# Modulation vectors of a two-block transformer: the weight tiles taken in four stages instead of one, part of each tile multiplied on TensorE

## The chip, the cores and the metric

The kernel runs on one core of a Trainium2 chip. The metric is the device time of one execution in microseconds (us); lower is better. Everything is computed in 32-bit floats. The core has five engines that run their own instruction lists and meet only at semaphores: TensorE (PE; loads of its weights are listed apart as PEld), VectorE (DVE), ScalarE (ACT), GpSimd (POOL) and SyncE (SP). SP and ACT issue the transfers of this kernel.

## The reference, cut to what matters

Two transformer blocks of two layers each work on x (512 tokens by 1024). Only the first block is modulated: six vectors for each layer come from one condition vector.

```python
cond = jax.nn.silu(c)                          # (1, 1024)
for layer in range(2):
    mod = cond @ w_ada[layer] + b_ada[layer]   # w_ada: (2, 1024, 6144)
    sh1, sc1, g1, sh2, sc2, g2 = jnp.split(mod[:, None, :], 6, axis=-1)
    h = rms_norm(x, norm_mix[layer]) * (1.0 + sc1) + sh1
    y = gated_deltanet_mixer(h, ...) if layer == 0 else dilated_attention_mixer(h, ...)
    x = x + g1 * y
    h = rms_norm(x, norm_ffn[layer]) * (1.0 + sc2) + sh2
    x = x + g2 * swiglu(h, w_ffn_in[layer], w_ffn_out[layer])
```

w_ada is 48 MB, the largest single input. It is a matrix times one vector: each of its numbers is used once.

## The kernel before

The program is a chain of **stages** (`Core.stage`). In each stage every engine has one list, written out by hand; no engine starts the next stage before all have ended this one. Within a stage the order on an engine is the order of the code, and it waits only where the code says `wait_ge`. x is kept turned, channels on partitions, as 8 tiles of 128x512.

**w_ada in tiles.** A tile is 512 columns of w_ada by all 1024 rows: 128 partitions by 8 row blocks k by 512 columns, 2 MB. There are 12 tiles for each layer. `set_up` takes all 24, one after the other, before anything else is computed. ACT loads them into six buffers (`tiles`, L362). DVE multiplies row block k by `cond[:, k]` and adds up over k, even and odd k in two separate sums (`scaled`, L401 and L404, eight instructions for a tile). TensorE adds over the 128 partitions by eight matmuls with one moving column of ones (L348). Also in `set_up`: x is loaded by one transfer and turned (L323, copied by L384), small vectors are loaded in rows by 28 or so transfers on SP and turned (L331, L387), the squares of x give the first root of the norm (L301, L338, L371).

**Decay rows** (`gdn_rows`) is the second stage: the norm of layer 0 (`Norm`: a diagonal on DVE L461, a spread by TensorE L448, eight products on DVE L455, eight shifts on ACT L443), a projection to 16 columns (L885, eight for the first half `part`, then eight for the second), then a chain between ACT and DVE over the decay rows (L899 to L940), a turn on TensorE (L891) and a copy (L942). `gdn_heads` follows, and its weights are requested at its start (L974). The rest of layer 0 follows and takes until 1162 us.

**Bias stage** (`window_biases`), the first of layer 1's mixer: four matmuls make bias rows (L1546), which go out to memory and come back shifted (L1535, L1539, into `slots[0]`); in the meantime the norm of layer 1 runs; then eight matmuls flip them (L1556), DVE copies each (L1571) and adds a mask (L1575).

**Dilated attention** (`window_attention`) goes over 12 pairs of heads m, each with four blocks of 128 queries (iterations r). For each m, SP loads three weight parts (keys, queries, values) into `slots[m % 2]` (L1633). In iteration r TensorE computes the scores of r (L1698), parts of the projections of pair m+1 and m+2 (L1650, L1659, L1666) with their sums of squares (L1677) and the spread of inverse roots (L1684), the attention of r-2 (L1712) and the turn of the probabilities of r-1 (L1724). DVE does `maxima(r)` (L1855, L1859), ACT the exponents (L1796), DVE `weigh(r)` (L1865, L1868).

## Time and profile before

| | us |
|---|---|
| three timed runs | 4657.93, 4659.88, 4664.34 |
| their median | 4659.88 |
| the profiled execution | 4659.29 |
| its span, first to last instruction | 4657.5 |
| set-up stage, to 156.48 | 156.5 |
| decay rows, 156.48 to 184.06 | 27.6 |
| TensorE busy | 4303.1 (92%) |
| DVE busy | 1943.2 (42%) |
| mean granted TensorE clock | 0.932 |

[...] A 32-bit matmul is two records in the trace, so "x16" in a timeline row is eight matmuls. A timeline row merges neighbours of one kind: start, duration of the merged piece, engine, line, operation, operands, shape, count of records, and in brackets the idle time before it and what ended it. "SPq" and "ACTq" are the issuing of transfers.

### The profile page before, as it was taken

Reading aid. Unit: us, or ns where it says so; the run is one execution under the profiler, and the core shown is the slowest. Engines: PE = TensorE matmul, PEld = TensorE weight load, DVE = VectorE, ACT = ScalarE, POOL = GpSimd, SP = SyncE. Lnnn points to the kernel's source line nnn. Section 1 sums busy time; section 2 is a strip of 40 time slices with the busy share of each in tenths; the row PEclk is TensorE's granted clock in tenths of the full one; section 3 lists DMA queues with packets and bytes.
Section 4 is the critical chain, followed back from the end, with each engine's and each line's share of the span. In section 5 each row is a group of like instructions: output and inputs, shape, how many; then the busy total and the mean of one; then the engine's idle time right before and its main releaser. Section 6 shows DMA issues by size and latency. Waiting matters only on the chain. (4 is left out here: it accounts for less than half of the span.)

```text
span 4657.5 us, 51781 instructions
## 1 busy us (share of the span) xinstructions
PE 4303.1 (92%) x18256; PEld 2930.7 (63%) x18256; DVE 1943.2 (42%) x3480; ACT 897.4 (19%) x1784; POOL 1022.3 (22%) x738
## 2 busy tenths in 40 slices
PE   6799799999899789988889999999899799999998
PEld 6444696888466378874554444888645544447887
DVE  7465543332233443322347012675223570127752
ACT  0233221100233211002340101221013401002210
POOL 0000322443100034420005000444200051004443
PEclk6799899999899799998989999999899899998998
DMA  9421002322222023244112221232351132222332
GB/s 374 135 57 36 5 14 77 90 80 75 74 55 55 10 81 88 84 97 90 35 39 72 72 72 54 81 90 84 72 105 30 35 81 72 63 63 72 90 86 68
DMA packets 621097, 351.02 MB, mean 75 GB/s; under 512 B 67890, under 2 KB 591091, under 8 KB 620964
## 3 DMA queue, kind: packets, MB, share of 16 engines
q1 hardware_dynamic: 593188, 297.12, 24.3%
q10 hardware_dynamic: 27776, 52.18, 3.0%
q8 instruction: 78, 1.28, 0.1%
q14 instruction: 55, 0.45, 0.0%
HBM read 339.77 MB, written 2.13 MB: 73 GB/s over the span
## 5 line engine op out<-in xcount | busy, mean ns | idle before, releaser
L676 PE MATMUL psum<-h_normed,weight_slot 128*128 128x256 f32 x2816 | 645.6, 383 | 16.9 <-DMA weight_slot<-in_ffn_w_up 7.9
L228 PE MATMUL psum<-h_normed,weight_slot 128*128 128x512 f32 x1408 | 610.0, 596 | 18.4 <-DMA weight_slot<-in_w_in 18.4
L676 PEld LDWEIGHTS psum<-h_normed,weight_slot 128*128 128x128 f32 x2816 | 540.5, 192 | 98.0 <-issue 23.1
L228 PEld LDWEIGHTS psum<-h_normed,weight_slot 128*128 128x128 f32 x1408 | 269.1, 191 | 357.5 <-issue 357.5
L676 PE MATMUL psum<-sums_in,weight_slot 128*128 128x256 f32 x2112 | 485.0, 379 | 5.6 <-POOL weight_slot L650 5.6
L644 POOL TENSOR_TENSOR weight_slot<-weight_slot 128x512 f32<-128x512 f32 (+1 forms) x136 | 173.2, 1273 | 1415.5 <-DMA weight_slot<-in_w_ffn_in 837.8
L676 PEld LDWEIGHTS psum<-sums_in,weight_slot 128*128 128x128 f32 x2112 | 400.9, 190 | 61.5 <-POOL weight_slot L650 7.2
L739 DVE COPY work<-psum 128x256 f32<-128x256 f32 x104 | 43.8, 421 | 618.7 <-PE psum L676 618.7
L2883 DVE SCALAR_TENSOR_TENSOR u<-raw,vectors,u 128x511 f32<-128x511 f32 (+1 forms) x176 | 214.9, 1240 | 99.7 <-ACT u L2862 86.6
L2144 PE MATMUL psum<-h_normed,weight_slot 128*128 128x512 f32 x576 | 252.5, 600 | 2.6 <-ACT o_swa L2333 2.6
L676 PE MATMUL psum<-sums_hidden,weight_slot 128*128 128x256 f32 x1056 | 243.8, 379 | 0.0
L983 PE MATMUL psum<-h_normed,weight_slot 128*128 128x512 f32 x512 | 232.6, 610 | 11.5 <-DMA weight_slot<-in_gdn_w_in 11.5
L676 PEld LDWEIGHTS psum<-sums_hidden,weight_slot 128*128 128x128 f32 x1056 | 200.5, 190 | 27.6 <-POOL weight_slot L650 0.5
L2144 PEld LDWEIGHTS psum<-h_normed,weight_slot 128*128 128x128 f32 x576 | 110.1, 192 | 141.6 <-issue 141.4
L650 POOL TENSOR_TENSOR weight_slot<-weight_slot 128x512 f32<-128x512 f32 (+1 forms) x136 | 185.8, 1366 | 10.7
L983 PEld LDWEIGHTS psum<-h_normed,weight_slot 128*128 128x128 f32 x512 | 98.3, 195 | 134.3 <-issue 134.3
L646 POOL TENSOR_TENSOR weight_slot<-weight_slot 128x512 f32<-128x512 f32 (+1 forms) x136 | 179.7, 1321 | 10.7
L648 POOL TENSOR_TENSOR weight_slot<-weight_slot 128x512 f32<-128x512 f32 (+1 forms) x136 | 179.5, 1320 | 10.7
L2729 POOL TENSOR_TENSOR x_residual<-x_residual,h_normed 128x512 f32<-128x512 f32 x16 | 19.9, 1272 | 714.9 <-DVE h_normed L2717 714.9
L676 PE MATMUL psum<-conv_ffn_hidden,weight_slot 128*128 128x256 f32 x704 | 160.1, 379 | 0.0
L676 PE MATMUL psum<-ffn_hidden,weight_slot 128*128 128x256 f32 x704 | 160.1, 379 | 0.0
L2635 DVE SCALAR_TENSOR_TENSOR o_conv<-padded,vectors,o_conv 128x512 f32<-128x512 f32 x240 | 159.2, 743 | 0.0
(395 smaller groups left out, 5883.5 us busy)
## 6 DMA issues: line engine op xcount, KB each, us to landing
tiles<-in_w_ada ACTq DMA_DIRECT2D x24, 2048.0 KB, 15.2
weight_slot<-in_w_ffn_in SPq DMA_DIRECT2D x88, 512.0 KB, 4.9
weight_slot<-in_ffn_w_up SPq DMA_DIRECT2D x88, 512.0 KB, 4.8
weight_slot<-in_w_gate SPq DMA_DIRECT2D x64, 512.0 KB, 4.7
weight_slot<-in_w_in SPq DMA_DIRECT2D x40, 512.0 KB, 4.9
weight_slot<-in_dsw_w_in SPq DMA_DIRECT2D x36, 512.0 KB, 5.4
weight_slot<-in_gdn_w_in SPq DMA_DIRECT2D x32, 512.0 KB, 6.7
weight_slot<-in_w_ffn_out SPq DMA_DIRECT2D x64, 256.0 KB, 3.5
```

Source lines behind the costliest of these rows:

```text
L228: last = c.nc.tensor.matmul(c.ps[:, 4 * s + t, :], weights(c.slots[s], t, k), moving(k), start=(k == 0), stop=(k == kt - 1))
L644: nc.gpsimd.tensor_tensor(b(self.S1), b(self.A21), b(self.A22), ALU.add).then_inc(self.folded, 1)
L646: nc.gpsimd.tensor_tensor(b(self.S2), b(self.S1), b(self.A11), ALU.subtract).then_inc(self.folded, 1)
L648: nc.gpsimd.tensor_tensor(b(self.S3), b(self.A11), b(self.A21), ALU.subtract).then_inc(self.folded, 1)
L650: nc.gpsimd.tensor_tensor(b(self.S4), b(self.A12), b(self.S2), ALU.subtract).then_inc(self.folded, 1)
L676: last = nc.tensor.matmul(c.ps[:, 4 * bank + r // 2, (r % 2) * self.HALF:(r % 2 + 1) * self.HALF], c.slots[s][:, b * 512 + k * P:b * 512 + ...
L739: nc.vector.tensor_copy(u4, p(self.P1)).then_inc(self.link, 1)
L983: last = nc.tensor.matmul(c.ps[:, t, :], c.slots[s][:, (t * KT + k) * P:(t * KT + k + 1) * P], c.h[:, k, :], start=(k == 0), stop=(k == KT ...
L2144: last = nc.tensor.matmul(c.ps[:, BANK_OF[t], :], c.slots[j % 2][:, (i * KT + k) * P:(i * KT + k + 1) * P], c.h[:, k, :], start=(k == 0), ...
L2635: nc.vector.scalar_tensor_tensor(o_conv[:, t, :], padded[:, t, ds(k, S)], c.vec[:, ds(layer * (CONVW * CT) + k * CT + (cw + t), 1)], o_con ...
L2729: nc.gpsimd.tensor_tensor(c.x[:, k, :], c.x[:, k, :], c.h[:, k, :], ALU.add).then_inc(self.pool_added, 1)
L2883: ins = nc.vector.scalar_tensor_tensor(u[:, s, t, back:], raw[:, s, t, 0:S - back], tap(i, s, t, 2 - back), u[:, s, t, back:], ALU.mult, A ...
```

## The change

- `c` is loaded by a transfer of its own, first on SP, and turned by one matmul into a bank of its own; the condition `c.cond` is now kept for the whole program. x is loaded by four transfers, one for 128 tokens each; its squares are summed on ACT.
- A tile's row blocks k = 0 to 4 are summed on DVE into one sum (`Modulation.sum_tile`: five instructions, each waiting for the one before it). For row blocks 5, 6, 7 TensorE takes the tile itself as weights and `cond[:, k]` as the one moving column (`Modulation.products`): with the sum's own matmul this makes 16 matmuls for a tile instead of 8.
- The tiles are taken in four stages: layer 0's first four (sh1, sc1) in `set_up`; its other eight in `gdn_rows`; layer 1's first four in `window_biases`; its other eight in `window_attention`, all eight row blocks on DVE there (`scale_part`, two instructions in each iteration r of the pairs m = 0 to 7), with four added matmuls for each pair m = 2 to 9 behind L1677.
- Layer 0's tiles go through a ring of seven buffers, which are the later `silu_z`, `q_decayed`, ... of the mixer. Tiles 0 to 6 are loaded by ACT, 7 to 10 by SP in `set_up`, 11 by SP in `gdn_rows`. In the bias stage ACT loads four tiles at its start. In dilated attention SP loads half tiles between the weights.
- The projection of `gdn_rows` goes over k outside and over the two halves inside, and the second half is written to PSUM partitions 64 to 71.
- The weights of the first pair of heads are requested at the end of SP's list in the bias stage (`first_window_weights`), and pair m uses `slots[(m + 1) % 2]`.

```diff
+            sp.dma_start(cond_rows[:, :], ins["c"].rearrange("a (k p) -> (a k) p", p=P)).then_inc(cond_loaded, 16)
+            sp.dma_start(c.ident[:, :], c.const("ident")).then_inc(cond_loaded, 16)
+            for t in range(TT):
+                sp.dma_start(x_rows[:, t, :], ins["x"][0, t * P:(t + 1) * P, :]).then_inc(x_loaded[t], 16)
...
+            for n in range(len(ring), ADA_FIRST + len(ring)):
+                sp.wait_ge(ada.multiplied, n - len(ring) + 1)
+                ada.load(sp, ring, n)
...
+            nc.tensor.transpose(c.ps[:, 7, 0:KT], cond_rows[:, :], c.ident[0:KT, 0:KT]).then_inc(cond_turned, 1)
...
+            for n in range(ADA_FIRST):
+                if n == 2:
+                    pe.wait_ge(vecs_loaded, 16 * len(loads))
+                    for b in range(2):
+
+                        pe.wait_ge(copied, b + 2)
+                        for t in range(4):
+                            last = nc.tensor.transpose(c.ps[:, b + 1, t * P:(t + 1) * P], vec_rows[:, 4 * b + t, :], c.ident[:, :])
+                        last.then_inc(turned, 1)
+                ada.products(pe, n, ring[n], n)
...
-            with pe.Fori(0, DEPTH * STEPS // 2) as i:
-                for s in range(2):
-
-                    pe.wait_ge(done, i * 2 + (s + 1 + ADA))
-                    for t in range(4):
-                        for part in range(2):
-                            last = nc.tensor.matmul(c.ps[:, 0, ds(i * 8 + (4 * s + t), 1)],
-                                                    scaled[:, s, part, t * P:(t + 1) * P], c.ones[:, 0:1],
-                                                    start=(part == 0), stop=(part == 1))
-                    last.then_inc(summed, 1)
...
-            with dve.Fori(0, DEPTH * STEPS // ADA) as i:
-                for s in range(ADA):
-                    n = i * ADA + s
-
-                    dve.wait_ge(loaded[s], i * 16 + 16)
-                    dve.wait_ge(summed, n + 1)
-                    for k in range(KT):
-
-                        to = scaled[:, s % 2, k % 2, :]
-                        if k < 2:
-                            ins = nc.vector.tensor_scalar(to, tiles[:, s, k, :], cond[:, k:k + 1], None, ALU.mult)
-                        else:
-                            dve.wait_ge(added, n * (KT - 1) + (k - 1))
-                            ins = nc.vector.scalar_tensor_tensor(to, tiles[:, s, k, :], cond[:, k:k + 1], to, ALU.mult, ALU.add)
-                        ins.then_inc(added if k < KT - 1 else done, 1)
...
+ADA_TILES = 12
+ADA_FIRST = 4
+ADA_REST = ADA_TILES - ADA_FIRST
+class Modulation:
+    SPLIT = 5
+    def __init__(self, c, sems, bank, scaled=None):
+        self.c, self.bank = c, bank
+        self.link, self.summed, self.multiplied = sems
+        self.scaled = c.slots[1][:, 3 * D:4 * D].rearrange("p (s n) -> p s n", s=2) if scaled is None else scaled
+    def load(self, engine, ring, n):
+        engine.dma_start(ring[n % len(ring)], columns(self.c.ins["w_ada"][n // ADA_TILES, :, :], n % ADA_TILES * 512, 512)
+                         ).then_inc(self.c.ada_loaded[n % len(ring)], 16)
+    def sum_tile(self, dve, i, tile):
+        c, nc = self.c, self.c.nc
+        to = self.scaled[:, i % 2, :]
+        if i >= 2:
+            dve.wait_ge(self.multiplied, i - 1)
+        nc.vector.tensor_scalar(to, tile[:, 0, :], c.cond[:, 0:1], None, ALU.mult).then_inc(self.link, 1)
+        for k in range(1, self.SPLIT):
+            dve.wait_ge(self.link, i * (self.SPLIT - 1) + k)
+            nc.vector.scalar_tensor_tensor(to, tile[:, k, :], c.cond[:, k:k + 1], to, ALU.mult, ALU.add
+                                           ).then_inc(self.link if k < self.SPLIT - 1 else self.summed, 1)
+    def products(self, pe, i, tile, place):
+        c, nc = self.c, self.c.nc
+        pe.wait_ge(self.summed, i + 1)
+        for t in range(4):
+            at, to = slice(t * P, (t + 1) * P), c.ps[:, self.bank, 4 * place + t:4 * place + t + 1]
+            for k in range(self.SPLIT, KT):
+                nc.tensor.matmul(to, tile[:, k, at], c.cond[:, k:k + 1], start=(k == self.SPLIT), stop=False)
+            last = nc.tensor.matmul(to, self.scaled[:, i % 2, at], c.ones[:, 0:1], start=False, stop=True)
+        last.then_inc(self.multiplied, 1)
+    def add_bias(self, dve, first, n, place):
+        c, b = self.c, self.c.column("b_ada")
+        return c.nc.vector.tensor_tensor(c.mod[:, 4 * first:4 * (first + n)], c.ps[:, self.bank, 4 * place:4 * (place + n)],
+                                         c.vec[:, b + 4 * first:b + 4 * (first + n)], ALU.add)
...
-            for part in range(2):
-                for k in range(KT):
-                    pe.wait_ge(norm.ready, k + 1)
-                    last = nc.tensor.matmul(c.ps[0:GH, part, :], w_ab[:, k, part * GH:(part + 1) * GH], c.h[:, k, :],
+            for k in range(KT):
+                pe.wait_ge(norm.ready, k + 1)
+                for part in range(2):
+                    last = nc.tensor.matmul(c.ps[64 * part:64 * part + GH, part, :], w_ab[:, k, part * GH:(part + 1) * GH], c.h[:, k, :],
                                             start=(k == 0), stop=(k == KT - 1))
-                last.then_inc(projected, 1)
+            last.then_inc(projected, 1)
+            for i in range(REST // 2):
+                ada.products(pe, i, tile_of(i), i)
 
             pe.wait_ge(rows_stacked, 4)
             for t in range(TT):
                 last = nc.tensor.transpose(c.ps[:, 2, t * P:(t + 1) * P], stacked[:, t * P:(t + 1) * P], c.ident[:, :])
             last.then_inc(turned, 1)
+            for i in range(REST // 2, REST):
+                ada.products(pe, i, tile_of(i), i)
...
+            for i in range(ADA_FIRST):
+                ada.products(pe, i, ring[i], i)
             norm.tensor(pe)
             pe.wait_ge(spread, 64)
 
-            pe.wait_ge(norm.ready, KT)
-            for h in range(WH):
+            for h in (0, 1, 2, 3, 6, 7, 5, 4):
 
                 if h < 4:
                     pe.wait_ge(copied, h + 1)
+                if h == 5:
+                    pe.wait_ge(biased, 1)
+                if h == 4:
+                    pe.wait_ge(norm.ready if norm.shift is None else norm.scaled, KT)
                 nc.tensor.matmul(c.ps[:, h, :], flip[:, :], falling[:, h, :, :].rearrange("p j n -> p (j n)"),
...
+            for i in range(ADA_FIRST):
+                act.dma_start(ring[i], columns(c.ins["w_ada"][1, :, :], i * 512, 512)).then_inc(c.ada_loaded[i], 16)
...
+            for i in range(ADA_FIRST):
+                dve.wait_ge(c.ada_loaded[i], 16 * (landed[i] + 1))
+                ada.sum_tile(dve, i, ring[i])
+            dve.wait_ge(ada.multiplied, ADA_FIRST)
+            ada.add_bias(dve, ADA_TILES, ADA_FIRST, 0).then_inc(biased, 1)
+            dve.wait_ge(biased, 1)
+            modulated_gain(c, 1, 0).then_inc(biased, 1)
+            dve.wait_ge(biased, 2)
             norm.vector(dve)
...
+            def load_half(j, half):
+                if j:
+                    sp.wait_ge(taken, 2 * (j - 1) + half + 1)
+                w = columns(c.ins["w_ada"][1, :, :], (ADA_FIRST + j) * 512, 512)
+                sp.dma_start(tile[:, half, :, :], w[:, half * (KT // 2):(half + 1) * (KT // 2), :]).then_inc(half_loaded[half], 16)
+
+            window_weights(c, sp, 1, w_loaded[1])
+            load_half(0, 0)
+            load_half(0, 1)
+            for m in range(2, NM):
+                sp.wait_ge(v_projected, m - 1)
+                if 3 <= m < ADA_REST + 2:
+                    load_half(m - 2, 0)
+                window_weights(c, sp, m, w_loaded[m % 2])
+                if 3 <= m < ADA_REST + 2:
+                    load_half(m - 2, 1)
...
+                if part == 1 and 2 <= m < ADA_REST + 2:
+                    last = sum_tile(m - 2)
                 last.then_inc(summed, 1)
+
+            def sum_tile(j):
+
+                pe.wait_ge(ada_summed, j + 1)
+                for t in range(4):
+                    last = nc.tensor.matmul(c.ps[:, SUMS, 16 + t:17 + t], scaled[:, j % 2, t * P:(t + 1) * P], c.ones[:, 0:1],
+                                            start=True, stop=True)
+                return last
...
+            def scale_part(r):
+                j, b = r // TT, r % TT
+                half = b // 2
+                to = scaled[:, j % 2, :]
+                if b % 2 == 0:
+                    dve.wait_ge(half_loaded[half], 16 * (j + 1))
+                if b == 0 and j >= 2:
+                    dve.wait_ge(summed, 2 * j + 2)
+                for k in range(2 * b, 2 * b + 2):
+                    col, row = c.cond[:, k:k + 1], tile[:, half, k % (KT // 2), :]
+                    if k == 0:
+                        nc.vector.tensor_scalar(to, row, col, None, ALU.mult).then_inc(ada_link, 1)
+                        continue
+                    dve.wait_ge(ada_link, j * KT + k)
+                    ins = nc.vector.scalar_tensor_tensor(to, row, col, to, ALU.mult, ALU.add).then_inc(ada_link, 1)
+                dve.wait_ge(ada_link, j * KT + 2 * b + 2)
+                if b % 2:
+                    dve.sem_inc(taken, 1)
+                if b == 3:
+                    dve.sem_inc(ada_summed, 1)
```

The helper `load` of `Modulation` is called by ACT and SP as described. Where the engines stand, at three places:

DVE in the decay rows, before (h_normed is the norm's result, work and decay_rows the decay chain, decay_cols its turned form):

```order
L461 TENSOR_TENSOR root<-ident,inverse_rms 128x512
L455 SCALAR_TENSOR_TENSOR h_normed<-x_residual,modulated_gains,psum 128x512 x8
L926 TENSOR_SCALAR work<-psum,scalars 8x512
L928 SCALAR_TENSOR_TENSOR work<-work 8x512
L930 TENSOR_SCALAR work<-work,scalars 8x512
L932 SCALAR_TENSOR_TENSOR decay_rows<-resets,work 8x512
L936 TENSOR_TENSOR work<-decay_rows 8x512
L940 TENSOR_TENSOR work<-decay_rows 8x512
L942 COPY decay_cols<-psum 128x128
```

DVE at the same place now, from the norm to the third tile (keys_beta_decay, keys_to_end and values_beta are three buffers of the ring, and weight_slot holds the sums):

```order
L468 SCALAR_TENSOR_TENSOR h_normed<-x_residual,modulated_gains,psum 128x512 x8
L404 TENSOR_SCALAR weight_slot<-keys_beta_decay,cond 128x512
L407 SCALAR_TENSOR_TENSOR weight_slot<-keys_beta_decay,cond,weight_slot 128x512 x4
L956 TENSOR_SCALAR work<-psum,scalars 8x512
L404 TENSOR_SCALAR weight_slot<-keys_to_end,cond 128x512
L407 SCALAR_TENSOR_TENSOR weight_slot<-keys_to_end,cond,weight_slot 128x512 x4
L959 SCALAR_TENSOR_TENSOR work<-work 8x512
L961 TENSOR_SCALAR work<-work,scalars 8x512
L963 SCALAR_TENSOR_TENSOR decay_rows<-resets,work 8x512
L967 TENSOR_TENSOR work<-decay_rows 8x512
L404 TENSOR_SCALAR weight_slot<-values_beta,cond 128x512
L407 SCALAR_TENSOR_TENSOR weight_slot<-values_beta,cond,weight_slot 128x512 x4
```

The fourth tile's sum follows behind L972, the turned copy L975 stands behind that, and the last four tiles follow L975.

SP in the bias stage and at the start of dilated attention, before (flip and the three above it are constants, bias_rows the rows in memory, in_dsw_w_in the weights of the heads):

```order
L1530 DMA table<-in_rel_bias 32x24
L1531 DMA hot<-in_constants 33x1024
L1532 DMA classmask<-in_constants 128x128
L1533 DMA flip<-in_constants 128x128
L1535 DMA bias_rows<-rows 8x4x256
L1539 DMA weight_slot<-bias_rows 128x8x128 x4
L186 UNCONDITIONAL_BRANCH
L1626 UNCONDITIONAL_BRANCH
L1633 DMA weight_slot<-in_dsw_w_in 128x8x128 x36
```

And now:

```order
L1578 DMA flip<-in_constants 128x128
L1580 DMA bias_rows<-rows 8x4x256
L1584 DMA weight_slot<-bias_rows 128x8x128 x4
L1653 DMA weight_slot<-in_dsw_w_in 128x8x128 x3
L189 UNCONDITIONAL_BRANCH
L1702 UNCONDITIONAL_BRANCH
L1653 DMA weight_slot<-in_dsw_w_in 128x8x128 x3
L1708 DMA tile<-in_w_ada 128x4x512 x2
L1653 DMA weight_slot<-in_dsw_w_in 128x8x128 x3
```

The first pair's three weight parts have moved ahead of the stage's end (the two branches), and half tiles stand between the others.

TensorE in iteration r = 6 of dilated attention (third block of the second pair), before:

```order
L1698 MATMUL psum<-k_two,q_two 128x128 x4
L1666 MATMUL psum<-weight_slot,h_normed 128x128 x8
L1677 MATMUL psum<-halves,square 128x2 x4
L1666 MATMUL psum<-weight_slot,h_normed 128x128 x8
L1712 MATMUL psum<-probs_t,v_rows 64x128 x2
L1724 MATMUL psum<-ident,probs 128x128 x4
```

And now:

```order
L1796 MATMUL psum<-k_two,q_two 128x128 x4
L1754 MATMUL psum<-weight_slot,h_normed 128x128 x8
L1765 MATMUL psum<-halves,square 128x2 x4
L1775 MATMUL psum<-ones,scaled 128x1 x4
L1754 MATMUL psum<-weight_slot,h_normed 128x128 x8
L1810 MATMUL psum<-probs_t,v_rows 64x128 x2
L1822 MATMUL psum<-ident,probs 128x128 x4
```

Four matmuls with one moving column are added behind the sums of squares, in one iteration of four, for eight pairs.

## Rows read from the trace of the kernel before

**Rows 1.** Busy us by stretch: PE, PEld, DVE, ACT, POOL; then PEclk, DMA share, GB/s.
```profile
29.00:31.00 2.00, 2.00 (x11) 2.00 (x11) 0.00 (x0) 0.00 (x0) 1.33 (x2) 0.50 1.05 410
...
140.00:150.00 10.00, 7.60 (x36) 7.44 (x35) 10.00 (x18) 0.00 (x0) 0.00 (x0) 0.50 0.01 4
```

**Rows 2.** Timeline, set-up, one tile: start, us, engine, line, work, [idle before].
```profile
142.09 0.88 DVE L401 TENSOR_SCALAR scaled<-tiles,cond 128x512 f32<-128x512 f32 x2
...
142.31 3.57 PE L348 MATMUL psum<-ones,scaled 128*128 128x1 f32 x16 [1.20 <-DVE scaled L404]
142.88 4.05 DVE L404 SCALAR_TENSOR_TENSOR scaled<-tiles,cond,scaled 128x512 f32<-128x512 f32 x6
...
156.48 0.39 SPq L869 DMA_DIRECT2D w_ab<-in_gdn_w_in  x1
```

**Rows 3.** What writes or reads the tiles: ns min/median/max; landing in us.
```profile
L404 DVE SCALAR_TENSOR_TENSOR scaled<-tiles,cond,scaled x144: 741/742/1529, 37.2 to 151.0; 128x512 f32<-128x512 f32 x144
...
DMA to landing us min/median/max: 7.6/15.2/19.8
```

**Rows 4.** Timeline, the start of set-up.
```profile
0.82 33.65 ACTq L362 DMA_DIRECT2D tiles<-in_w_ada  x6
...
18.87 3.08 DVE L384 COPY x_residual<-psum 128x512 f32<-128x512 f32 x5 [0.16 <-PE psum L323]
```

**Rows 5.** Timeline, decay rows.
```profile
157.27 2.07 PE L448 MATMUL psum<-root,ones 128*128 128x512 f32 x2 [1.85 <-DVE root L461]
159.38 5.36 DVE L455 SCALAR_TENSOR_TENSOR h_normed<-x_residual,modulated_gains,psum 128x512 f32<-128x512 f32 x8 [2.17 <-PE psum L448]
...
161.02 16.13 PE L885 MATMUL psum<-h_normed,w_ab 128*8 128x512 f32 x32 [1.68 <-ACT h_normed L443]
...
182.29 1.11 PE L891 MATMUL psum<-ident,stacked 128*128 128x128 f32 x4 [5.14 <-ACT stacked L918]
...
184.06 0.27 SPq L965 DMA_DIRECT2D hot<-in_constants  x1
```

**Rows 6.** DMA issues: count, KB each, median us from issue to landing.
```profile
weight_slot<-in_dsw_w_in SPq DMA_DIRECT2D x36, 512.0 KB, 5.4
...
ident<-in_constants SPq DMA_DIRECT2D x1, 64.0 KB, 2.0
ones<-in_constants SPq DMA_DIRECT2D x1, 64.0 KB, 5.2
```

**Rows 7.** Timeline, bias stage and the first projection of dilated attention.
```profile
1163.38 0.42 SPq L1533 DMA_DIRECT2D flip<-in_constants  x1
...
1165.58 3.58 PE L1546 MATMUL psum<-hot,table 33*8 33x256 f32 x8 [4.27 <-DMA flip<-in_constants]
...
1180.76 9.79 PE L1556 MATMUL psum<-weight_slot,flip 128*128 128x512 f32 x16 [8.42 <-DMA weight_slot<-bias_rows]
...
1191.31 1.23 DVE L1575 TENSOR_TENSOR biases<-biases,classmask 128x1024 f32<-128x1024 f32 x1
1192.87 7.54 SPq L1633 DMA_DIRECT2D weight_slot<-in_dsw_w_in  x6
...
1200.62 10.10 PE L1650 MATMUL psum<-h_normed,weight_slot 128*128 128x512 f32 x16 [10.07 <-DMA weight_slot<-in_dsw_w_in]
```

**Rows 8.** Busy time by stretch: one pair of heads in dilated attention.
```profile
1264.00:1295.00 31.00, 31.00 (x186) 19.77 (x186) 11.57 (x24) 11.29 (x28) 0.00 (x0) 1.00 0.19 52
```

**Rows 9.** Timeline within the same pair of heads.
```profile
1270.79 7.13 PE L1659 MATMUL psum<-h_normed,weight_slot 128*128 128x512 f32 x16
...
1281.34 0.95 PE L1677 MATMUL psum<-halves,square 128*128 128x2 f32 x8
...
1284.22 2.93 SPq L1633 DMA_DIRECT2D weight_slot<-in_dsw_w_in  x3
...
1285.84 0.88 DVE L1855 SCALAR_TENSOR_TENSOR psum<-psum,root,biases 128x256 f32<-128x256 f32 x2 [2.67 <-PE psum L1698]
...
1291.06 1.08 PE L1684 MATMUL psum<-diagonal,ones 128*64 128x512 f32 x4
```

More of the change, by code:

```diff
@@ L368, in _ @@
-            nc.scalar.activation(cond[:, :], c.vec[:, cc:cc + KT], ACT.Silu).then_inc(cond_ready, 1)
-            act.wait_ge(taken, KT)
-            act.wait_ge(cleared, 2)
-            nc.scalar.activation(c.small[:, 0, :], c.ps[:, 7, 0:TT], ACT.Sqrt, bias=c.eps[:, :], scale=1.0 / D).then_inc(rooted, 1)
-            for i in range(1, STEPS // ADA):
-                load(0, i)
-            for layer in range(1, DEPTH):
-                with act.Fori(0, STEPS // ADA) as i:
-                    load(layer, i)
+            for n in range(ADA_FIRST):
+                ada.load(act, ring, n)
@@ L422, in modulation, with modulated_gain @@
+def modulated_gain(c, layer, half):
+    g = c.column(("norm_mix", "norm_ffn")[half], layer * KT)
+    m = layer * 48 + (1, 4)[half] * KT
+    o = (layer * 2 + half) * KT
+    return c.nc.vector.scalar_tensor_tensor(c.gains[:, o:o + KT], c.mod[:, m:m + KT], 1.0, c.vec[:, g:g + KT], ALU.add, ALU.mult)
 def modulation(c, layer, part):
@@ L1885, in _ @@
                     invert(m + 1)
+                if m < ADA_REST:
+                    scale_part(r)
                 weigh(r)
```

195 lines of the change are left out of this document (106 added, 89 removed).

## The prediction, made before the changed kernel ran

> **What bounds the kernel now.** I read the busy time by stretch first, then the timeline of the stages that the change touches, because the chain that ended last only covers the final microseconds. Set-up lasts 156.5 us [rows 2] and is bound by VectorE: over 140 to 150 it is busy 10.00 of 10.00 us, TensorE waits for it in every tile, and transfers are long over (DMA share 0.01) [rows 1]. A tile costs VectorE eight instructions, 4.05 us plus 0.88 us less their overlap; tiles follow each other some 4.8 us apart, and TensorE needs 3.57 us of that for eight matmuls (16 records) [rows 2]. One such matmul costs 0.446 us. [...] The decay rows (27.6 us) are a chain over four engines, the bias stage ends on TensorE's flips and VectorE's copies, and dilated attention is TensorE without a gap: 31.00 of 31.00 us at clock 1.00, with VectorE busy 11.57 [rows 5, 7, 8].
>
> So the change takes VectorE's work off set-up and puts more on TensorE, at half clock, where a tile now costs 16 x 0.446 = 7.14 us. On VectorE it costs one multiply (0.44, half of 0.88 [rows 2]) and four multiply-adds, each waiting for the last; one lasts 742 ns [rows 3] and I add 0.04 for the wait: 3.6 us. Bounds for the multiply-add are the overlapped 4.05 / 6 = 0.675 and about 1. With two sums buffered, 3.6 hides under 7.14, and **TensorE becomes the bound of every tile outside dilated attention**.
>
> **Set-up, by time.** x's turned copies ended at 18.87 + 3.08 = 21.95 before [rows 4]. x still shares the transfers with two to four tiles, and ACT is held while it issues tiles (six took it 33.65 us, most of that a wait for the vectors [rows 4]); the condition needs only a small early transfer, so I leave 22.0. First sum ends at 25.6. Four tiles 28.6; eight turns of the vectors at half clock, twice 1.11 [rows 5], 2.2; bias, gain and the change of stage 1.1. Set-up ends at 57.5 instead of 156.5: **-99.0**.
>
> **Decay rows.** The transfer of `w_ab` now stands on SP's queue behind tile 10, which is requested only when the last product of set-up is done, at 56.4. A tile's landing takes at least 7.6 us [rows 3], and a small load beside tiles takes 5.2 where one alone took 2.0 [rows 6]; I put `w_ab` at 66.0, 8.5 us into the stage, where before the projection began 4.5 us in [rows 5]. The projection itself, 16 matmuls in 16.13 us before, now has its halves in different column groups. A pair of such matmuls, 64 columns each and 512 wide, took 1.08 us together [rows 9] where one 512-wide matmul takes 7.13 / 8 = 0.89; so eight pairs cost 6.9 to 8.6 at full clock, I take 9.1 with the cold start, and 16.1 if nothing overlaps. It ends at 75.1. TensorE then does four tiles (28.6), the turn of the rows with its copy (1.5), waits for the fifth sum, which stands behind that copy on VectorE (3.6, nothing hides it), and does four more (28.6); end 0.9. Nothing of the decay chain comes late: it needs some 14 us from the projection and has 28.6. The stage ends at 138.3 and takes 80.8 us instead of 27.6: **+53.2**. Tiles arrive every 5.1 us (2 MB at the 410 GB/s of [rows 1]), less than 7.14, so transfers are hidden.
>
> **Bias stage.** Its constants share the queue engines with four tiles of ACT: flip's landing, 2.2 us after issue before [rows 7], becomes 5.2 [rows 6], so the bias rows end 3.0 later, at 1172.7. First sum 3.6, then four tiles 28.6: 1204.9. All this now stands ahead of the norm of layer 1, which before ran while the bias rows were in memory: bias and gain 0.6, diagonal 0.8, spread 2.2, eight products 5.4 [rows 5], then eight copies of 0.68 and the mask 1.23 [rows 7], change of stage 0.4, together 16. The flips fit under the norm except the last. End at 1220.9 instead of 1192.9: **+28.0**. The bias rows' way through memory (until 1180.8) is hidden either way.
>
> **Dilated attention.** Its first weights are there at the start: TensorE waited from 1192.87 to 1200.62 [rows 7], of which 0.3 stays: **-7.4**. The first eight matmuls took 10.10 cold and take 7.13 warm [rows 7, 9]; whether the clock stays up over the change of stage no row shows: 0 to -3.0, I take **-1.5**. Added on TensorE: four matmuls for each of eight pairs, priced like the sums of squares of L1677, 0.95 less its tail, 0.9 [rows 9]: **+7.2**, fully exposed since the engine has no gap. On VectorE two multiply-adds, 1.6 us, in each iteration: it idles 2.67 us or more before each `maxima` [rows 9], so they cost nothing; without that cover they would cost up to 1.6 x 32 = 51 us. On SP the half tiles stand between the weights: a pair's weights are asked for at 1284.2 [rows 9] and used a pair (31 us) later, a half tile 11 us later. Last bias and gain at the end: **+0.7**.
>
> **The sum** is -99.0 + 53.2 + 28.0 - 7.4 - 1.5 + 7.2 + 0.7 = -18.8 us. Against the profiled execution's 4659.29 (span 4657.5 and 1.8 around it) that is 4640.5; the median shown is 0.6 above that execution, so **4641**.
>
> [...] What a full clock would give is the first rival.
>
> **Rivals.**
> 1. *The clock rises in the tiles.* TensorE then takes 3.57 us for a tile and VectorE's 3.6 or the transfer's 5.1 binds. Set-up ends 14.6 earlier; the decay rows then wait for the last tiles and end about 21 earlier still, the bias stage 12.8: together 49, 4592. [...]
> 2. *The constants come last.* In the bias stage they land only when ACT's four tiles have: 1162.3 + 7.6 + 3 x 5.1 = 1185.2 instead of 1168.6, all behind it 16.6 later: 4657, no difference to be measured. For it: one small load took 5.2 instead of 2.0 with tiles in flight. Against it: that was with two tiles in flight, and it was not 15. It decides from about 10 us on.
> 3. *Slower: VectorE stalls in dilated attention on a half tile.* `scale_part` waits for the transfer ahead of `weigh(r)` and of the next `maxima`, which scores and exponents hang on. VectorE can be late by 2.67 - 1.6 = 1.1 us before anything moves [rows 9], so a half tile that lands more than 12 us after its request begins to push. At 3 us for each of 16 halves that is 48: 4689. It needs landings over twice those that weights of half its size show, 5.4 us for 512 KB [rows 6], on queues with a share of 0.19 [rows 8].
>
> **How the numbers follow.** Forecast as above: 0.78. Rival 1: 0.05; rival 2: 0.12; rival 3: 0.05. About 0.2% (9.3 us) is what a measurement of this kernel can tell from no change: below 4650.6 is faster, above 4669.2 slower. The forecast's own bounds are the projection without overlap (+7.0), the clock (+1.5 or -1.5), the multiply-adds where they are exposed (5 sums, +4), and downwards a first product at full clock or a shorter start (-8 in all): 4629 to 4654, which lies beyond 4650.6 in a small part. Faster 0.81, same 0.13, slower 0.06. The range that leaves out rivals 1, 3 and half of rival 2 is 4625 to 4656.
>
> **What would show it.** Right: set-up ends near 57 us and the decay rows near 138; 32 records of products in 7.1 us at clock 0.50; TensorE waits once for a sum, about 3.6 us, in the middle of the decay rows; the bias stage is 28 us longer; the pairs m = 2 to 9 take 0.9 us longer each and VectorE's idle time there shrinks by 1.6 an iteration. Wrong: a granted clock of 1.00 in the products, a projection of 16 us, TensorE waiting in dilated attention for VectorE or for tiles.

## The result, and the profile after

| | before | changed kernel |
|---|---|---|
| median of the timed runs, us | 4659.99 (4656.78 to 4664.34, six) | 4640.89 (4635.89 to 4645.02, six) |
| span of the profiled execution | 4657.5 | 4642.2 |
| TensorE / DVE busy | 4303.1 / 1943.2 | 4314.4 / 1924.8 |

The ratio is 0.9959 with an interval of 0.9947 to 0.9972: faster, by 19.1 us. 4641 was forecast. The totals of the page say why a count of busy time would have foretold nothing: TensorE has 11 us more and DVE 18 less, of some 4650.

```profile
PE 4314.4 (93%) x18385; PEld 2949.0 (64%) x18385; DVE 1924.8 (41%) x3435; ACT 903.1 (19%) x1800; POOL 1015.7 (22%) x730
```

The time went where the stages begin and end. A stage's mark is the first transfer that SP issues in it; where SP is still held, it is the first work of another engine (dilated attention in the changed kernel: TensorE at 1174.91):

| stage | before, us long | after | moved | forecast |
|---|---|---|---|---|
| set-up | 156.5 | 58.1 | -98.4 | -99.0 |
| decay rows | 27.6 | 80.3 | +52.7 | +53.2 |
| rest of layer 0, untouched | 978.1 | 978.2 | +0.1 | 0 |
| bias stage | 30.7 | 58.2 | +27.5 | +28.0 |
| dilated attention | 382.4 | 381.5 | -0.9 | -1.0 |
| the rest, untouched | 3082.2 | 3085.8 | +3.6 | 0 |

Timeline of the changed kernel, the set-up and the start of the decay rows. They answer to [rows 2], [rows 4] and [rows 5]; columns as there.

```profile
9.61 7.01 ACTq L396 DMA_DIRECT2D l_transposed<-in_w_ada  x1
16.65 1.28 ACT L345 ACT_TABLE_LOAD   x1 [16.65 <-issue]
...
24.44 0.45 DVE L404 TENSOR_SCALAR weight_slot<-silu_z,cond 128x512 f32<-128x512 f32 x1
24.93 3.11 DVE L407 SCALAR_TENSOR_TENSOR weight_slot<-silu_z,cond,weight_slot 128x512 f32<-128x512 f32 x4
...
28.19 1.41 PE L416 MATMUL psum<-cond,silu_z 128*128 128x1 f32 x6 [6.25 <-DVE weight_slot L407]
29.46 0.56 PE L417 MATMUL psum<-ones,weight_slot 128*128 128x1 f32 x2
29.89 1.42 PE L416 MATMUL psum<-cond,silu_z 128*128 128x1 f32 x6
...
58.11 2.76 SPq L891 DMA_DIRECT2D w_ab<-in_gdn_w_in  x1
...
60.92 3.50 SPq L892 DMA_DIRECT2D resets<-in_constants  x1
...
64.46 2.05 SPq L893 DMA_DIRECT2D scalars<-in_gdn_a_log  x1
...
66.55 0.29 SPq L894 DMA_DIRECT2D scalars<-in_gdn_dt_bias  x1
...
70.60 9.34 PE L910 MATMUL psum<-h_normed,w_ab 128*8 128x512 f32 x32 [9.64 <-DMA scalars<-in_gdn_dt_bias]
79.87 0.83 PE L416 MATMUL psum<-cond,keys_beta_decay 128*128 128x1 f32 x6
80.56 0.36 PE L417 MATMUL psum<-ones,weight_slot 128*128 128x1 f32 x2
...
110.22 1.44 PE L416 MATMUL psum<-cond,q_decayed 128*128 128x1 f32 x6 [3.92 <-DVE weight_slot L407]
...
138.44 0.27 SPq L1004 DMA_DIRECT2D hot<-in_constants  x1
```

In the rows of 28 to 30 us, four matmuls (three with the tile as weights, one with the sum: 6 and 2 records) are followed by the next four 1.70 us later, 28.19 to 29.89. That is 0.427 us for one matmul, 6.83 for a tile. After the projection, at 79.87, the same four take 0.91. The sum on DVE is 0.45 + 3.11 = 3.6 us, from 24.44 to 28.04.

Windows of the changed kernel (columns as in [rows 1]; they answer to its rows and to [rows 8]):

```profile
30.00:40.00 10.00, 10.00 (x49) 10.00 (x48) 5.01 (x8) 0.00 (x0) 0.00 (x0) 1.00 1.06 405
...
80.00:90.00 10.00, 10.00 (x57) 10.00 (x58) 9.58 (x14) 7.58 (x9) 0.00 (x0) 0.60 0.41 136
90.00:100.00 10.00, 10.00 (x48) 10.00 (x48) 5.00 (x8) 1.89 (x3) 0.00 (x0) 0.50 0.19 75
...
1220.00:1251.00 31.00, 31.00 (x187) 19.77 (x185) 16.44 (x31) 11.30 (x28) 0.00 (x0) 1.00 0.40 119
```

TensorE is the bound of every tile, as forecast: busy 10.00 of 10.00 while DVE has half its time free. The column behind POOL, PEclk, is the clock granted to TensorE as a share of full speed. The first row shows 1.00 there, but 49 records in 10 us is the same rate as the 48 at 0.50 in the third. In this trace the clock is shown as 1.00 up to 82 us, and a stretch ahead of that is better read by what one matmul takes. TensorE is busy 10.00 of 10.00 at 0.50 again in the last four tiles of the decay rows:

```profile
120.00:130.00 10.00, 10.00 (x48) 10.00 (x48) 4.41 (x7) 0.00 (x0) 0.00 (x0) 0.50 0.00 0
```

In dilated attention TensorE is still without a gap and DVE's busy time in 31 us went from 11.57 [rows 8] to 16.44.

Timeline, bias stage and the start of dilated attention (they answer to [rows 7]):

```profile
1116.68 0.36 SPq L1575 DMA_DIRECT2D table<-in_rel_bias  x1
...
1118.13 0.45 SPq L1578 DMA_DIRECT2D flip<-in_constants  x1
1124.74 3.58 PE L1592 MATMUL psum<-hot,table 33*8 33x256 f32 x8 [9.22 <-DMA flip<-in_constants]
...
1132.37 1.44 PE L416 MATMUL psum<-cond,ada_tiles 128*128 128x1 f32 x6 [4.05 <-DVE weight_slot L407]
...
1162.89 7.64 PE L1607 MATMUL psum<-weight_slot,flip 128*128 128x512 f32 x16
...
1174.91 8.52 PE L1738 MATMUL psum<-h_normed,weight_slot 128*128 128x512 f32 x16 [4.37 <-PEq L189]
```

The last row starts with the stage. Before, it stood 7.4 us behind that and took 10.10.

### The profile page after: what moved, and what is told of

It is laid out like the page before. It is cut to its first block and busy times, and to the rows that moved or that the text cites. A ratio compares the mean times of both kernels' runs of the same rounds, so it can differ in the third digit from the quotient of the medians.

```text
span 4642.2 us, 51706 instructions
## 1 busy us (share of the span) xinstructions
PE 4314.4 (93%) x18385; PEld 2949.0 (64%) x18385; DVE 1924.8 (41%) x3435; ACT 903.1 (19%) x1800; POOL 1015.7 (22%) x730
## 5 line engine op out<-in xcount | busy, mean ns | idle before, releaser
L689 PEld LDWEIGHTS psum<-sums_hidden,weight_slot 128*128 128x128 f32 x1056 | 200.6, 190 | 27.5 <-POOL weight_slot L663 0.3
L663 POOL TENSOR_TENSOR weight_slot<-weight_slot 128x512 f32<-128x512 f32 (+1 forms) x136 | 185.4, 1363 | 10.7
L661 POOL TENSOR_TENSOR weight_slot<-weight_slot 128x512 f32<-128x512 f32 (+1 forms) x136 | 180.6, 1328 | 10.7
L659 POOL TENSOR_TENSOR weight_slot<-weight_slot 128x512 f32<-128x512 f32 (+1 forms) x136 | 180.1, 1324 | 10.7
```

Of the source, the lines that this page charges most:

```text
L659: nc.gpsimd.tensor_tensor(b(self.S2), b(self.S1), b(self.A11), ALU.subtract).then_inc(self.folded, 1)
L661: nc.gpsimd.tensor_tensor(b(self.S3), b(self.A11), b(self.A21), ALU.subtract).then_inc(self.folded, 1)
L663: nc.gpsimd.tensor_tensor(b(self.S4), b(self.A12), b(self.S2), ALU.subtract).then_inc(self.folded, 1)
L689: last = nc.tensor.matmul(c.ps[:, 4 * bank + r // 2, (r % 2) * self.HALF:(r % 2 + 1) * self.HALF], c.slots[s][:, b * 512 + k * P:b * 512 + ...
```

## The experiments

All are edits of the changed kernel. split6, split8 and wab_act were measured beside its repetition, `after_again`, where the kernel before took 4662.06 us. The others were measured later, when it took 4659.06 (early_split6, warm, unpacked, dve_double) and 4660.78 (best, weights_late, no_att_products); there the ratio, which is always to the kernel before, and the stages count for more than the difference of two totals.

**after_again**, nothing edited.

> The changed kernel once more, unchanged, as the measure for the runs beside it: 4641, with some 4 us either way from one execution to the next. If the later, untouched stages are responsible for the 3.5 us by which its first profile's span is longer than my sum, their time should differ again here while set-up (58.1), decay rows (to 138.4) and bias stage (58.2 long) stay within 0.5 us.

4642.66 us (4640.76 to 4646.83), ratio to before 0.9957, interval 0.9940 to 0.9974. The stages came out at 58.3, 79.1, 58.2 and 380.1 us (set-up, decay rows, bias stage, dilated attention). So a stage of its own can move by 1.4 us between executions; in dilated attention the whole of it is in the first eight wide matmuls, 7.11 us here and 8.52 above (more on them at weights_late):

```profile
1174.88 7.11 PE L1738 MATMUL psum<-h_normed,weight_slot 128*128 128x512 f32 x16 [3.34 <-PEq L189]
```

Therefore the comparisons below rest on stage lengths where a total says too little: the untouched stretch between decay rows and bias stage took 977.9 to 983.7 us over the thirteen profiles of this study, and the untouched rest behind dilated attention 3081.2 to 3087.7.

**split6**, one row block less for TensorE, one more for DVE.

```
-    SPLIT = 5
+    SPLIT = 6
```

> Six row blocks of a tile on VectorE, two on TensorE, instead of five and three. Theory (TensorE at 0.427 us a matmul binds every tile): 12 matmuls, 5.1 us a tile instead of 6.8, less 0.8 for each of three sums that nothing hides: set-up to about 52, decay rows' eight tiles 13 us shorter, bias stage 6 shorter, in all about 19 less than the changed kernel: 4622. The projection in the decay rows still starts near 70, since the w_ab transfer waits for the tiles ahead of it in the queue. Rival (the transfers bind, at 5.1 us a tile): set-up and decay rows gain under 5, only the bias stage gains, in all 4632 or more.

4627.88 us (4627.60 to 4630.94), ratio 0.9925, interval 0.9908 to 0.9941: 14.8 below the repetition. The direct price of a row block on TensorE is confirmed in the bias stage: 52.6 us instead of 58.2, with 16 matmuls fewer (6.8 at 0.427; the first sum starts TensorE 0.8 later). In the decay rows (73.9 us, from 80.3 and 79.1) only 5 to 6.5 of the expected 13 came, since the projection still began at 70.7, and set-up ended at 55.7, not 52. The timeline shows what stood in the way:

```profile
52.07 3.16 SPq L396 DMA_DIRECT2D l_transposed<-in_w_ada  x1
...
52.28 0.17 DVE L432 SCALAR_TENSOR_TENSOR modulated_gains<-modulation,vectors 128x8 f32<-128x8 f32 x1
55.71 5.29 SPq L891 DMA_DIRECT2D w_ab<-in_gdn_w_in  x1
...
55.74 0.69 DVE L474 TENSOR_TENSOR root<-ident,inverse_rms 128x512 f32<-128x512 f32 x1 [3.29 <-PEq L189]
```

DVE is done with set-up at 52.45 and the next stage starts 3.3 us later, when SP has got rid of tile 10, which it could not hand over for 3.16 us. After that the next small transfer holds SP for 5.29. So theory and rival were both partly right: TensorE sets the tiles, and transfers set where the projection starts.

**split8**, all eight row blocks on DVE, TensorE only adds over partitions (`SPLIT = 8`, and the sum's matmul with `start=True`).

> All eight row blocks on VectorE, TensorE left with four matmuls a tile. Theory: VectorE binds with 0.49 + 7 x 0.77 = 5.9 us a tile, TensorE adds 1.7 only at the end of a row of tiles; 0.9 a tile less than now over 16 tiles, set-up to about 53, decay rows to 132, bias stage 6 shorter: 4629, faster than the changed kernel that gives TensorE a part. Rival (TensorE's part is a help): slower than 4641, by up to 16 x 2.3 = 37 us, since VectorE has 2.3 us more in each tile.

4628.90 us (4626.57 to 4633.51), ratio 0.9929, interval 0.9912 to 0.9946. The theory holds, and the rival, slower than the change, falls.

```profile
30.34 0.48 DVE L404 TENSOR_SCALAR weight_slot<-q_decayed,cond 128x512 f32<-128x512 f32 x1
30.86 5.48 DVE L407 SCALAR_TENSOR_TENSOR weight_slot<-q_decayed,cond,weight_slot 128x512 f32<-128x512 f32 x7
```

A tile now costs DVE 6.0 us, 0.78 for each multiply-add that waits for the last, and TensorE 1.7. That is less than the 6.83 that TensorE alone takes for a tile in the change. **The part of the change that takes tiles to TensorE directly costs 11 to 14 us** (the three stages with such tiles are 10.7 to 11.7 shorter, the median is 13.8 lower); none of the gain comes from it. split6 and split8 are 1.0 us apart, which is less than either spreads. DVE pays 0.78 for a row block and TensorE four times 0.427 = 1.71 at half clock.

**wab_act**, the four small transfers at the start of the decay rows issued by ACT instead of SP, since SP is held there.

```
-            sp.dma_start(w_ab[:, :, :], columns(w, GCH + GHK, 2 * GH)).then_inc(loaded, 16)
-            (and resets, gdn_a_log, gdn_dt_bias)
+            act.dma_start(...) for the same four, ahead of norm.scalar(act)
```

> The four small transfers of the decay rows are issued by ScalarE, whose queue is empty then, instead of by SyncE behind two tiles. Theory (queue order held the projection): it starts at about 63 instead of 70.6, all behind it moves along, 7 us less: 4634. Rival (tile bandwidth held it): no change, since the queue engines are still full until 65.

4637.39 us (4636.53 to 4645.16), ratio 0.9945, interval 0.9928 to 0.9961, which overlaps that of the repetition. The stages decide, and they speak for the rival:

```profile
59.55 0.31 ACTq L925 DMA_DIRECT2D scalars<-in_gdn_dt_bias  x1
...
68.52 4.44 PE L906 MATMUL psum<-h_normed,w_ab 128*8 128x512 f32 x10 [7.61 <-DMA scalars<-in_gdn_dt_bias]
```

The last transfer leaves 7.0 us earlier than in the change (59.55, not 66.55) and lands 2.1 earlier: 9.0 us after its issue, where 4.0 were enough for the one that SP issued at 66.55. Tile 10, issued at 57.26 by SP in the changed kernel, landed at 69.7. So which engine issues them is worth 2.1 us of the 7.0; that the tiles in flight hold the rest is what early_split6 puts to the test.

**early_split6**: split6, and the same four transfers issued by SP in set-up, ahead of the tiles 7 to 10, with a semaphore and buffers of their own (the rows of x stand in `h_normed` to make room).

```
+            sp.dma_start(w_ab[:, :, :], columns(c.ins["gdn_w_in"][0, :, :], GCH + GHK, 2 * GH)).then_inc(c.rows_loaded, 16)
+            (and the other three)
             for n in range(len(ring), ADA_FIRST + len(ring)):
                 sp.wait_ge(ada.multiplied, n - len(ring) + 1)
```

> split6 with the four small transfers of the decay rows issued in set-up, ahead of SyncE's four tiles (x's rows lie in the place of h_normed to make room). Theory, after the run in which ScalarE issued them gained only 2.1 us at the projection: it is the tiles in flight that hold any small transfer asked for after them, so one asked for before them does not wait. The projection then starts about 5 us after the stage does, near 60 instead of 70.7, TensorE is held next by tile 4's sum, and the decay rows end 9 us earlier than in split6, near 120: 4619. Rival (the tiles themselves then come late, since they have the same bytes to bring): the gain is under 4 us and TensorE or VectorE waits for a tile.

4614.59 us (4607.43 to 4617.51), ratio 0.9902, interval 0.9885 to 0.9918. In its waits TensorE waits for no small transfer any more; the one ahead of the projection (L914) is the norm's:

```profile
PE psum L914 <- ACT h_normed L463: 1.7, 1, 1.7
```

The projection begins at 61.3 instead of 70.7, and the stage ends at 121.1 instead of 129.6. It begins some 4.5 us into its stage, as before the change. That is 8.5 us for issuing four transfers earlier, and the rival's late tiles did not come.

**warm**: two unused 128x512 matmuls per tile are added, behind the third and the eleventh of its sixteen own. The edit asks two things: whether the price of a narrow matmul follows the granted clock, and whether wide work holds that clock at 1.00. If both held, the author expected 5.1 us a tile and 4615 to 4625 in all.

```
+            if t % 2 == 0:
+                nc.tensor.matmul(c.ps[:, 6, :], c.ident[:, :], tile[:, KT - 1, :], start=True, stop=True)
             last = nc.tensor.matmul(to, self.scaled[:, i % 2, at], c.ones[:, 0:1], start=False, stop=True)
```

> The changed kernel with two added matmuls of 128x512 in each tile outside dilated attention, whose result is not used. [...] Rival (the narrow ones are slow for another reason than the clock): the two wide ones come on top at 1.7 each, 3.4 a tile over 16 tiles, near 4695; or at full clock 0.86 each, near 4668.

4686.96 us in one run. Of the decay rows, where the granted clock was 1.00 over 89 to 90 us and 0.50 over 97 to 98:

```profile
89.50 1.10 PE L418 MATMUL psum<-keys_beta_decay,ident 128*128 128x512 f32 x2
...
93.22 0.81 PE L416 MATMUL psum<-cond,keys_beta_decay 128*128 128x1 f32 x6
...
97.14 1.42 PE L416 MATMUL psum<-cond,keys_to_end 128*128 128x1 f32 x6
...
100.13 2.05 PE L418 MATMUL psum<-keys_to_end,ident 128*128 128x512 f32 x2
...
90.00:100.00 10.00, 10.00 (x54) 8.24 (x52) 9.61 (x15) 7.99 (x10) 0.00 (x0) 0.73 0.47 160
...
110.00:120.00 10.00, 10.00 (x37) 7.93 (x36) 0.00 (x0) 0.00 (x0) 0.00 (x0) 0.50 0.01 2
```

The first holds here: the price of such a matmul follows the clock, 0.81 for three at 1.00 against 1.42 at 0.50, and a tile with its two wide matmuls took 5.31 us at full clock and 10.24 at half. The second does not: two wide matmuls a tile did not hold the clock. TensorE was busy 1.00 of 1.00 us over 94 to 95, where the mean fell to 0.78, and 10.00 of 10.00 over 110 to 120 at 0.50, and the kernel paid for the added work at the low clock, up to 3.4 us for each of the sixteen tiles outside dilated attention.

**unpacked**: both halves of the projection to PSUM partitions 0 to 7 again (`c.ps[0:GH, part, :]`).

> [...] Theory (the two halves ran side by side): the projection takes 16 us instead of 9.3, the decay rows end 6.7 later, near 145. Rival (the new order over k alone made it short): no change.

4648.39 us in one run. The decay rows end at 145.5 instead of 138.4 (137.4 in the repetition), 7.1 to 8.1 later.

```profile
70.75 16.55 PE L910 MATMUL psum<-h_normed,w_ab 128*8 128x512 f32 x32 [10.01 <-DMA scalars<-in_gdn_dt_bias]
```

So the halves written to partitions 0 to 7 and 64 to 71 do run beside each other: 9.34 us, against 16.55 with both at 0 to 7, each with eight columns of weights of 32 bits. The forecast had taken 9.1 and 16.1 from other rows.

**dve_double**: in dilated attention a second multiply-add into a spare row ahead of each one of `scale_part`, to see how much cover DVE has there.

```
+                    nc.vector.scalar_tensor_tensor(spare[:, :], row, col, row, ALU.mult, ALU.add).then_inc(again, 1)
```

> The changed kernel with VectorE's part in dilated attention done twice: each multiply-add of scale_part is preceded by another into a spare row, 0.75 us, 64 in all, 48 us of work. Theory (that work lies in VectorE's idle time, which is 2.3 us or more before each maxima): most of it is still hidden; dilated attention, 381.5 us long, grows by 0 to 5. Rival (VectorE's added work already costs something there): it grows by 1.5 us in each of 32 iterations, 48.

4646.62 us in one run; dilated attention took 379.7 us, not more than the 381.5 and 380.1 of the change.

```profile
1220.00:1251.00 31.00, 31.00 (x180) 19.74 (x179) 21.77 (x40) 11.30 (x28) 0.00 (x0) 1.00 0.40 119
```

DVE works 5.3 us more in 31 than in the change, 1.3 an iteration, and TensorE still has no gap: neither the change's work on DVE there nor as much again costs anything. The total is above the repetition only in stages that the edit doesn't touch: its stretch ahead of the bias stage took 982.7.

**no_att_products**: the four matmuls with one moving column are left out of each of the pairs m = 2 to 9, so layer 1's last eight tiles are summed but never added over partitions.

> The changed kernel without the four matmuls for each of eight pairs in dilated attention; layer 1's last eight tiles are summed on VectorE but never added over the partitions, so that part of the modulation is left out. Theory (exposed on a TensorE without gaps, 0.9 for each pair): the stage is 7.2 shorter, 374.3 instead of 381.5. Rival (the stage is longer for VectorE's or the transfers' sake): under 3.

4637.82 us in one run; dilated attention took 374.0, against 381.5 and 380.1: the 32 matmuls cost 6 to 7.5 us. The first eight wide matmuls took 8.80 here, 8.52 and 7.11 in those two; with that difference taken out both comparisons give 7.8, all of it exposed.

**weights_late**: the first pair's weights are asked for at the start of dilated attention, as before the change.

```
-            first_window_weights(c, sp)            (end of the bias stage)
+            first_window_weights(c, sp)            (start of dilated attention)
             window_weights(c, sp, 1, w_loaded[1])
```

> The changed kernel with the first pair's weights asked for at the start of dilated attention again. Theory: the wait of the kernel before comes back, 7.7 us between the start of that stage and its first matmul, and those matmuls run at half clock again, 10.1 instead of 8.5: the stage is 391 us long instead of 381.5. Rival: with the half tiles' transfers around, it is longer than that.

4654.27 us in one run; dilated attention took 389.6, 8.0 to 9.5 more.

```profile
1185.88 8.77 PE L1738 MATMUL psum<-h_normed,weight_slot 128*128 128x512 f32 x16 [11.43 <-DMA weight_slot<-in_dsw_w_in]
```

The first matmul began 7.8 us into the stage instead of at once, and that is the same in either comparison; the rest is the clock of the first eight, 8.77 us against 8.52 in one profile of the change and 7.11 in the other. It looks as if the longer stop had cost nothing at the clock, but the windows say otherwise. The first row is of the changed kernel, the next two of weights_late, the last two of the kernel before:

```profile
1175.00:1184.00 9.00, 9.00 (x18) 3.99 (x19) 0.08 (x1) 0.53 (x2) 8.77 (x10) 0.85 0.97 285
...
1174.00:1186.00 12.00, 0.57 (x3) 0.12 (x1) 3.90 (x7) 0.00 (x0) 7.53 (x9) 0.71 0.60 162
1186.00:1195.00 9.00, 9.00 (x18) 3.94 (x19) 0.00 (x0) 0.31 (x1) 7.31 (x8) 0.82 1.12 339
...
1193.00:1200.00 7.00, 0.00 (x0) 0.00 (x0) 0.07 (x1) 0.00 (x0) 6.77 (x8) 0.50 0.96 251
1200.00:1211.00 11.00, 10.38 (x18) 4.44 (x19) 0.00 (x0) 0.25 (x1) 8.07 (x9) 0.70 0.52 127
```

In all three the first of these matmuls ran at 0.50. By the means of windows of 1 us the clock stood at 0.50 for 2.9 us after the first matmul in the changed kernel, for 3.3 in weights_late and for 6.0 before the change, where the eight took 10.10 [rows 7]. In the repetition (7.11) it was 1.00 throughout. So behind the stop the clock was down to 0.50 in weights_late too, but for 3.3 us and not 6.0; why for less is not settled by this run.

**best**: early_split6, and (1) the fifth tile's sum on DVE ahead of the copy of the turned rows, (2) the bias stage's constants issued by ACT ahead of its tiles.

```
             sum_tile(dve, 3)
+            sum_tile(dve, REST // 2)
             dve.wait_ge(turned, 1)
```

> early_split6 with two more edits. (1) In the decay rows VectorE sums the fifth tile ahead of the turned copy, not behind it: TensorE's one long wait in the middle of the eight tiles, 4.4 plus the copy, goes, since that sum needs only the third tile's products: 4 to 5 us. (2) In the bias stage ScalarE issues the four constants ahead of its four tiles, instead of SyncE beside them: they then land near 3.5 us after the stage's start instead of 8.3, and the first sum is held by its tile's landing, near 9.5 to 10 instead of 12.2: 2 to 3 us. Together 6 to 8 less than early_split6 (its decay rows to 121.1, bias stage 52.4 long): 4607. Rival for (2): the tiles land so much later behind the constants that the first sum is no earlier.

4611.97 us (4606.10 to 4615.56), ratio to before 0.9888, interval 0.9872 to 0.9905. (1) is right: the decay rows end at 115.5 instead of 121.1, and one of the five waits for a sum is gone:

```profile
PE psum L423 <- DVE weight_slot L414: 12.0, 4, 7.0
```

(16.5 us in five in early_split6.) (2) gave nothing in the end:

```profile
1097.71 3.58 PE L1596 MATMUL psum<-hot,table 33*8 33x256 f32 x8 [4.50 <-DMA flip<-in_constants]
...
1104.46 0.49 DVE L411 TENSOR_SCALAR weight_slot<-ada_tiles,cond 128x512 f32<-128x512 f32 x1 [2.72 <-DMA ada_tiles<-in_w_ada]
```

The constants are there 4.9 us earlier in the stage, and the first sum begins 10.4 us into it instead of 12.6. But DVE now waits 2.72 us for the first tile, and 1.92 and 2.48 for the third and the fourth, which it did not have to wait for in early_split6; the bias stage took 53.5 us, some 1 more than there. The rival (tiles late behind the constants, the first sum no earlier) was right in its cause and in the outcome, not about the first sum. The two totals (4611.97 and 4614.59, measured at different times) differ by less than their spread, so (1) rests on its stage.

## Why the prediction was right

The mechanism, the signs and the stages' sizes came out as forecast; up to the end of dilated attention the sum is -18.9 against -18.8. That the two agree to 0.1 us is luck: within the stages there were misses of up to 5 us, and they cancelled.

- **Set-up** (-98.4; forecast -99.0). The step "the condition needs only a small early transfer, so I leave 22.0" failed: ACT, which computes the condition, was held until 16.65 by issuing two of its tiles (7.71 and 7.01 us; single issues of up to 5.0 us stood in the trace of before, and the forecast put this at nothing), x's copies on DVE stood behind the condition, and the first sum ended at 28.0 instead of 25.6. Working the other way, the price of a matmul was 0.427 instead of 0.446, which gives back 0.3 a tile. The trace of before had that price too: 0.446 was 3.57 / 8 with the last one's tail in it, while 64 records of the same form in a row took 13.65 us there, 0.427 for one.
- **Decay rows** (+52.7; forecast +53.2). `w_ab` and its companions were the most mis-sized term. SP was held 2.76, 3.50 and 2.05 us while issuing them, and the projection began at 70.6, not 66.0. The projection took 9.34 (9.1), the wait for the fifth sum 3.92 (3.6). Eight tiles at 0.3 less (2.4), the first two groups of four matmuls at full clock (1.6) and the stage's start 0.6 later than forecast repaid the 4.6.
- **Bias stage** (+27.5; forecast +28.0). `flip` landed 6.6 us after its issue, not 5.2, and the bias rows came 4.6 us later in the stage instead of 3.0; four tiles at the lower price took 1.2 back, and what follows the tiles took 15.0, not 16. The second rival, constants landing behind ACT's four tiles, did not happen, although the landings of 6.6 here and 9.0 in wab_act show the cause at work.
- **Dilated attention** (-0.9; forecast -1.0). weights_late puts the early weights at 7.8 for the wait (forecast -7.4) and 0.3 to 1.7 for the clock. Against before, the clock's term (-1.5) measured 1.6 and 3.0 in the two profiles (8.52 and 7.11 instead of 10.10), but weights_late had 1.3 of that without the early weights, which is not explained. no_att_products has 7.8 for +7.2. DVE waited for tiles not at all, so the third rival is out, and dve_double shows a cover larger than the 1.1 us that the forecast had granted.
- **The first rival**, a rising clock, is out too. The changed kernel's row of 90 to 100 us has TensorE busy 10.00 of 10.00 at 0.50; its 48 records are 24 matmuls at 0.42 us each, where the few at full clock took 0.23. [rows 1] had already shown the form of L338 at 0.50 while TensorE was busy 2.00 of 2.00. Being busy did not raise the clock for this form of matmul: it read 0.50 over the 27 us without a gap from 110.2 on, and in warm over 130 to 170 us (40.00 of 40.00 busy), even with two wide matmuls in 18.
- **The rest** was put at nothing and came out at +3.6 in this profile. It is in code that is word for word the same, its spread over thirteen profiles is 6.5 us, and the medians differ by 19.1, as the stages do. So it is counted as variation; nothing here explains it further.

What the prediction did not ask is whether the direct part on TensorE was worth having. It wrote "**TensorE becomes the bound of every tile**" and took that as the cost, when the same rows (0.78 for a row block on DVE, 1.71 on TensorE) price the alternative: split8 is 13.8 us below the repetition, split6 14.8.

Nor did it ask what the moving of the tiles is worth by itself. Two side edits carry most of the 19.1 us: with the projection's halves in the same columns again the decay rows end 7.1 to 8.1 later (unpacked), and with the first weights asked for late dilated attention is 8.0 to 9.5 longer (weights_late). Each was taken back by itself, never both together; if they add up, everything else in the change brought only some 1 to 4 us of the 18.9. The forecast's own terms say the same: without its 7.0 for the projection and its 7.4 and 1.5 for the weights, -2.9 is left of -18.8. With the tiles at six to two or eight to none, 11 to 15 us more come in.

## What to carry to other kernels

A matrix times one vector can be shared out between two engines by the price of a row block on each, and the shares should be sized so that both end together with the transfer: five to three was far from it (6.8 us on TensorE, 3.6 on DVE, 5.1 for the transfer). Six to two (5.1 on TensorE) balances better on paper, but was no faster than eight to none (6.0 on DVE) by more than the spread, where waits at the ends of the stages and for small transfers count as well. Work that is spread over other stages brings along small transfers that stand behind its large ones; issue those early (8.5 us here); issuing them from another engine brought 2.1. Where all work of a stage moves, forecast it by its marks, and check in the result that errors didn't merely cancel. Side edits that ride along with a change deserve a run of their own: here they were most of it.

## What the runs showed of the hardware that was not expected

- **Full and cold.** TensorE with 32-bit matmuls of one moving column, without any gap, was granted 0.50, and a clock that was 1.00 after the projection was back at 0.50 two us into them, at 82 (mean 0.60 over 80 to 90, 0.50 from 90 on). A matmul of that form takes 0.427 us at 0.50 and about 0.23 at 1.00.
- **The cold start varies.** The same eight wide matmuls at the start of dilated attention took 7.11 us in one profile of the changed kernel (after 3.34 without work) and 8.52 in another (after 4.37), 8.77 in weights_late (after 11.43) and 10.10 before the change (after 10.07). The granted clock was 1.00 throughout the first, and 0.50 for the first 2.9, 3.3 and 6.0 us of the others. The length of the stop alone does not order them.
- **A small transfer beside 2 MB ones** landed after 4.0 to 9.0 us, where one took 2.0 alone [rows 6], and issuing it held SP for up to 5.29 us in split6 and 6.81 in split8, as issuing a tile did (up to 7.71 on ACT). ACT was late for its own work in this way: it came to the condition at 16.65 us, behind the issues of 7.71 and 7.01.
- **The clock's record** does not fit the price of the work at the start: in the changed kernel it reads 1.00 up to 82 us, though a record of the projection took 1.06 us from 70.6 to 73 and 0.59 from 75.5 on. In split6 it reads 0.50 over 70.7 to 74 and 1.00 from 76 on, with the same 1.06 and 0.59.
